# Fp32r pairs in place of fp32 products in the recurrence of an RWKV-7 mixer: bonus, spread of the key norms, and v by token

## The reference

```
kk = heads(k * k_k);  kk = kk / max(sqrt(sum(kk * kk, -1)), 1e-12)
k = k * (1 + (a - 1) * k_a)
y = wkv7_scan(r, decay, k, v, -kk, kk * a)     # S = S diag(w) + (S a) b^T + v k^T ; y = S r
yn = ((y - mean(y)) * rsqrt(var(y) + GN_EPS)) * lnx[0] + lnx[1]
bonus = sum(r * k * r_k, -1) * v               # per head
out = ((yn + bonus) * g) @ w_out
```

## Time and profile before

| | |
|---|---|
| median of 3 runs | 3334.22 us (3332.93 to 3335.73) |
| the profiled execution | 3333.84 us, its span 3332.1 us |
| PE busy | 98% of the span |
| DVE, ACT busy | 54%, 37% |
| mean granted PE clock | 0.994 |
| the stage of the pairs | from 2604 us to 2799 us of the span |

### The profile page before, as it was taken

The page is one execution under the profiler, slowest core; times in us unless marked ns, Lnnn a source line. Parts: engine busy times, 40 slices in busy tenths (PEclk is TensorE's granted clock), DMA queues, the critical chain, the costliest instruction groups (busy, mean ns, idle before and its releaser), DMA issues.

```text
span 3332.1 us, 46863 instructions
## 1 busy us (share of the span) xinstructions
PE 3253.6 (98%) x20502; PEld 2658.2 (80%) x20502; DVE 1783.3 (54%) x2116; ACT 1216.2 (37%) x1534; POOL 97.2 (3%) x100
## 2 busy tenths in 40 slices
PE   8999998999999999999999999999999999999998
PEld 6877786888878888988788887888777787788886
DVE  5446665777354434454644347443476665754437
ACT  3346643323232222343332235222235554332224
POOL 2000000000000001000100011000000000100001
PEclk9999999999999999999999999999999999999999
DMA  5211231222222222222222222222222100122231
GB/s 194 77 51 51 76 114 63 89 101 86 96 97 101 90 94 108 102 89 89 95 90 97 89 104 84 95 101 87 90 70 75 47 4 16 70 101 101 86 104 64
DMA packets 45979, 286.47 MB, mean 86 GB/s; under 512 B 5952, under 2 KB 6224, under 8 KB 19920
## 3 DMA queue, kind: packets, MB, share of 16 engines
q1 hardware_dynamic: 44240, 280.34, 23.9%
q0 software_dynamic: 1536, 3.15, 0.4%
HBM read 278.22 MB, written 2.10 MB: 84 GB/s over the span
## 4 chain that ended last, share of the span: by engine, by line
PE 79%; DVE 5%; ACT 2%; issue 1%; DVEq 0%; ACTq 0%
PE ps L510 70%; PE ps L3189 3%; PE ps L3227 1%; PE ps L1217 1%; DVE wl L331 1%; PE ps L983 1%; DVE xl L2663 1%; PE ps L1218 0%; PE ps L1219 0%; ACT wh L315 0%; PE ps L2493 0%; DVE xl L1077 0%; PE ps L837 0%; DVE tmp L2671 0%; PE ps L3234 0%
## 5 line engine op out<-in xcount | busy, mean ns | idle before, releaser
L510 PE MATMUL ps<-xh,wh 128*128 128x512 f32 (+1 forms) x2464 | 966.3, 392 | 22.4 <-DVE xl L1077 10.5
L510 PE MATMUL ps<-xl,wh 128*128 128x512 f32 (+1 forms) x2464 | 946.2, 390 | 0.3
L510 PE MATMUL ps<-xh,wl 128*128 128x512 f32 (+1 forms) x2464 | 920.5, 391 | 0.0
L331 DVE TENSOR_TENSOR wl<-raw,wh 128x2048 fp32r<-128x2048 f32 (+1 forms) x284 | 591.2, 2082 | 452.5 <-ACT wh L315 452.3
L315 ACT CAST wh<-raw 128x2048 fp32r<-128x2048 f32 (+2 forms) x281 | 487.6, 1735 | 296.5 <-PE ps L510 290.2
L510 PEld LDWEIGHTS ps<-xh,wh 128*128 128x128 f32 (+1 forms) x2464 | 462.6, 188 | 131.8 <-issue 27.8
L510 PEld LDWEIGHTS ps<-xl,wh 128*128 128x128 f32 (+1 forms) x2464 | 462.3, 188 | 100.7 <-DVE xl L1077 2.8
L510 PEld LDWEIGHTS ps<-xh,wl 128*128 128x128 f32 (+1 forms) x2464 | 461.9, 188 | 99.4 <-issue 1.0
L510 PE MATMUL ps<-hid_h,wh 128*128 128x512 f32 x880 | 342.8, 390 | 0.0
L510 PE MATMUL ps<-hid_l,wh 128*128 128x512 f32 x880 | 342.4, 389 | 0.0
L510 PE MATMUL ps<-hid_h,wl 128*128 128x512 f32 x880 | 342.4, 389 | 0.0
(11 more groups left out here) (424 smaller groups left out, 4015.2 us busy)
## 6 DMA issues: line engine op xcount, KB each, us to landing
raw<-in_up SPq DMA_DIRECT2D x88, 1024.0 KB, 4.7
raw<-in_down SPq DMA_DIRECT2D x64, 704.0 KB, 4.0
raw<-in_up_c SPq DMA_DIRECT2D x22, 1024.0 KB, 4.8
raw<-in_down_c SPq DMA_DIRECT2D x16, 704.0 KB, 4.1
raw<-in_gates SPq DMA_DIRECT2D x8, 1024.0 KB, 4.7
raw<-in_gv SPq DMA_DIRECT2D x8, 1024.0 KB, 4.7
raw<-in_gu SPq DMA_DIRECT2D x8, 1024.0 KB, 4.7
raw<-in_gout SPq DMA_DIRECT2D x8, 1024.0 KB, 4.7
```

The source lines that it names most:

```text
L331: nc.vector.tensor_tensor(wl[:, slot, 0:w], raw[:, slot, 0:w], wh[:, slot, 0:w].bitcast(F32), ALU.subtract).then_inc(lo_ready, 1)
L510: last = nc.tensor.matmul(out, stationary, moving, start=(fresh and q == 0), stop=(t == kt - 1 and half == per - 1 and q == 2), skip_group ...
```

## The change: what it does

- The three products become pairs of fp32r products: the table (0, 1 and 1/64 entries) rounded once, the data in a high and a low part. `bonus` and `spread` issue two fp32r products of 512 columns each, `tokens_v` eight of 128 columns, with the parts of v as the weights.
- The parts: per pair ScalarE gets `value_high` (behind `decays(m+1)`) and `terms_high` (behind `lower(m+1)`), VectorE gets `value_low` (behind `operand_k(m+1)`) and `terms_low` (behind `add_x(m, 1)`). All use the same two buffers `part_h`, `part_l`. The key norms are split once: ScalarE's copy waits for the reciprocal, VectorE's subtraction follows it, both in `between[0]` of rv2.
- The rounded tables are made by ScalarE in the lead part: `picks_r` (128x256) first, `sums_r` (128x256) last. `spread(0)` waits for the first, `tokens_v(0)` for the second.
- The four buffers of parts lie in the slot of `raw` that held the last chunk of rv2. The load of the first rout chunk into that slot is held until the last pair's `bonus` product; the loads queued behind it on SyncE wait with it.

```diff
-               split_ahead=False, second_ahead=False, joint=False, paired=False, third=False):
+               split_ahead=False, second_ahead=False, joint=False, paired=False, third=False, hold=False):
...
-            for n in range(a, a + count):
+            for n in range(a, a + count - 1 if hold else a + count):
...
+        halves_r = place("halves_r", [P, 4, T], F32R, offset=raw_at + other * SLOT * 4)
+        part_h, part_l, norms_h, norms_l = (halves_r[:, n, :] for n in range(4))
...
+            def value_low(m):
+                need(dve, aH, m, "v")
+                mark(nc.vector.tensor_tensor(part_l, tile(v, m), part_h.bitcast(F32), ALU.subtract), vH, "v")
+
+            def terms_low(m):
+                need(dve, aH, m, "rkr")
+                mark(nc.vector.tensor_tensor(part_l, tile(r, m), part_h.bitcast(F32), ALU.subtract), vH, "rkr")
...
+            def value_high(m):
+                if m:
+                    need(act, pA, m - 1, "bonus")
+                mark(nc.scalar.copy(part_h, tile(v, m)), aH, "v")
+
+            def terms_high(m):
+                need(act, vL, m, "rkr")
+                need(act, pA, m, "v_tok")
+                mark(nc.scalar.copy(part_h, tile(r, m)), aH, "rkr")
...
+                masks_here(act)
+                nc.scalar.copy(picks_r[:, :, :], const[:, CONST["pick_low"]:CONST["pick_high"] + P].rearrange(
+                    "p (a c) -> p a c", a=2)).then_inc(tables_made.sem, 1)
                 key_scale(0)
                 unscaled_keys(0)
                 decays(0)
+                value_high(0)
+                act.wait_ge(kn_norm.sem, kn_norm.base + 5)
+                nc.scalar.copy(sums_r[:, :, :], const[:, CONST["heads"]:CONST["centre"] + P].rearrange(
+                    "p (a c) -> p a c", a=2)).then_inc(tables_made.sem, 1)
...
-                mark(nc.tensor.matmul(ps[:, bank["spread"], :], table("pick_low" if m < 4 else "pick_high")[rows, :],
-                                      key_norms[rows, :], start=True, stop=True), pS, "spread")
+                out, picks = ps[:, bank["spread"], :], picks_r[rows, m // 4, :]
+                nc.tensor.matmul(out, picks, norms_h[rows, :], start=True, stop=False)
+                mark(nc.tensor.matmul(out, picks, norms_l[rows, :], start=False, stop=True), pS, "spread")
...
+                need(pe, vH, m, "v")
                 for j in range(PAIRS):
                     at_ = slice(j * P, (j + 1) * P)
-                    last = nc.tensor.matmul(ps[:, bank["v_tok"], at_], tile(v, m)[:, at_], table("centre"), start=True, stop=True,
-                                            skip_group_check=True)
+                    for n, part in enumerate((part_h, part_l)):
+                        last = nc.tensor.matmul(ps[:, bank["v_tok"], at_], part[:, at_], sums_r[:, 1, :], start=(n == 0),
+                                                stop=(n == 1), skip_group_check=True)
...
-                need(pe, vL, m, "rkr")
-                mark(nc.tensor.matmul(ps[:, bank["bonus"], :], table("heads"), tile(r, m), start=True, stop=True), pA, "bonus")
+                need(pe, vH, m, "rkr")
+                nc.tensor.matmul(ps[:, bank["bonus"], :], sums_r[:, 0, :], part_h, start=True, stop=False)
+                mark(nc.tensor.matmul(ps[:, bank["bonus"], :], sums_r[:, 0, :], part_l, start=False, stop=True), pA, "bonus")
...
-                pe.wait_ge(kn_norm.sem, kn_norm.base + 3)
+                pe.wait_ge(kn_norm.sem, kn_norm.base + 5)
+                pe.wait_ge(tables_made.sem, tables_made.base + 1)
                 spread(0)
...
+        def norms_of_keys_high(act):
+            root_keys(act)
+            act.wait_ge(kn_norm.sem, kn_norm.base + 3)
+            nc.scalar.copy(norms_h, key_norms[:, :]).then_inc(kn_norm.sem, 1)
...
+            dve.wait_ge(kn_norm.sem, kn_norm.base + 4)
+            nc.vector.tensor_tensor(norms_l, key_norms[:, :], norms_h.bitcast(F32), ALU.subtract).then_inc(kn_norm.sem, 1)
...
+        @block.sync
+        def _(sp):
+            sp.wait_ge(pA.sem, pA.done(KD - 1, "bonus"))
+            load(sp, first["rout"])
```

More of the change, by code:

```diff
@@ L237, in _build @@
     at[0] = (at[0] + LINE - 1) // LINE * LINE
+    raw_at = at[0]
     raw = place("raw", [P, 2, SLOT])
@@ L2761, in rwkv @@
         kn_square, kn_sum, kn_norm = roles("keys_squared", "keys_summed", "keys_normed")
-        for s, n in ((kn_square, KD), (kn_sum, 1), (kn_norm, 3)):
+        for s, n in ((kn_square, KD), (kn_sum, 1), (kn_norm, 5)):
             s.stage(1, n)
@@ L2845, in rwkv @@
         head_sums = area("head_sums", [P, 2, 32], 82 * KB + 512)
+        halves_r = place("halves_r", [P, 4, T], F32R, offset=raw_at + other * SLOT * 4)
+        part_h, part_l, norms_h, norms_l = (halves_r[:, n, :] for n in range(4))
+        sums_r, picks_r = area("sums_r", [P, 2, P], 80 * KB, F32R), area("picks_r", [P, 2, P], 82 * KB + 768, F32R)
+        tables_made, = roles("sum_tables_rounded")
+        tables_made.stage(2, 1)
         masks_here = fetch([(reset[:, :], io["reset"]), (masks[:, :, :].rearrange("p m c -> p (m c)"), io["wmask"]),
@@ L2852, in rwkv @@
         vA = Named(sem("grams_vector"), ["x0", "rb_t", "ak_t", "rk_t", "bonus"], KD, lead=True)
+        aH = Named(sem("highs_scalar"), ["v", "rkr"], KD, lead=True)
+        vH = Named(sem("lows_vector"), ["v", "rkr"], KD, lead=True)
         vB = Named(sem("levels_vector"), ["add1", "add2", "add3", "add4", "add5"], KD, lead=True)
@@ L3009, in pair_vector @@
             if lead:
-                for s in (vE, vL, vA, vB, vC):
+                for s in (vE, vL, vA, vB, vC, vH):
                     dve.sem_inc(s.sem, s.per)
@@ L3015, in pair_vector @@
                 unit_keys(0)
+                value_low(0)
                 return
@@ L3031, in pair_vector @@
                 add_x(m, 1)
+                terms_low(m)
                 bonus(m)
@@ L3038, in pair_vector @@
                     operand_k(m + 1)
+                    value_low(m + 1)
                 add_x(m, 3)
@@ L3130, in pair_scalar @@
             if lead:
-                for s in (aE, aA, aB, aC):
+                for s in (aE, aA, aB, aC, aH):
                     act.sem_inc(s.sem, s.per)
+                masks_here(act)
+                nc.scalar.copy(picks_r[:, :, :], const[:, CONST["pick_low"]:CONST["pick_high"] + P].rearrange(
+                    "p (a c) -> p a c", a=2)).then_inc(tables_made.sem, 1)
                 key_scale(0)
@@ L3142, in pair_scalar @@
             lower(0)
+            terms_high(0)
             key_scale(1)
@@ L3157, in pair_scalar @@
                     decays(m + 1)
+                    value_high(m + 1)
                 turned_x(m, 2)
@@ L3174, in pair_scalar @@
                     lower(m + 1)
+                    terms_high(m + 1)
                 if next_:
@@ L3334, in pair_tensor @@
             pe.wait_ge(psum_read.sem, values_read)
+            pe.wait_ge(tables_made.sem, tables_made.base + 2)
             tokens_v(0)
@@ L3399, in rates_and_keys @@
             invert_keys(dve)
-        linear("rv2", KD, 256, x_split, dve_part=to_tiles(v[:, 4:KD, :], 2),
-               between={0: (root_keys, rates_and_keys),
+            dve.wait_ge(kn_norm.sem, kn_norm.base + 4)
+            nc.vector.tensor_tensor(norms_l, key_norms[:, :], norms_h.bitcast(F32), ALU.subtract).then_inc(kn_norm.sem, 1)
+        linear("rv2", KD, 256, x_split, dve_part=to_tiles(v[:, 4:KD, :], 2), hold=True,
+               between={0: (norms_of_keys_high, rates_and_keys),
                         1: (lambda act: pair_scalar(act, True), lambda dve: pair_vector(dve, True))},
```

## The result

The changed kernel takes 3346.51 us (median of 4 runs, 3346.03 to 3348.39), the kernel before 3334.09 (4 runs, 3332.93 to 3335.73). The ratio is 1.004, 95% interval 1.0028 to 1.0051: 12.4 us slower, where 3334.1 was forecast, within 3330.0 to 3338.0. The profiled execution took 3348.39 us, its span is 3346.6, 14.5 more than before.

What follows compares the result with a forecast made beforehand. TensorE's queue was taken to bound the pairs (21.86 of 22.4 us busy). Later unit 1 +1.9, lower clock +1.6 and shorter pairs -3.6 gave -0.1 us on 3334.22: 3334.1 us, range 3330.0 to 3338.0.

Steps and rivals of the forecast that it cites:

- the last sentence on the covers: SyncE: first rout chunk loads at the last bonus, about 2773, each chunk taking 4.7 us, split at 2799.32; cost nothing.
- The products: In each pair, bonus and spread take 0.65 us each (0.41 and 0.40 less), tokens_v 1.09 (0.10 more).
- the wait that was named: At xt(2) TensorE waits 0.25 us for VectorE's add, so spread saves only 0.15 of 0.40 us.
- Pair 0: The first pair, waiting on ScalarE's z copies already, was taken to get 0.4 us shorter.
- The last pair's 0.41: Saving of 0.41 us in the last pair, which has no spread and no tokens_v behind its bonus.
- The covers on ScalarE and VectorE: Making the parts of the data, about 0.6 to 0.69 us each, hides in idle time or behind other work; cost nothing.
- the margin called the narrowest: On ScalarE, terms_high (0.6 us) hides in 0.47 us of idle before turned_x(0) plus 0.29 before the z(1) copy.
- The rival of ScalarE as the bound: terms_high and value_high not hidden, each adding 0.5 us a pair: 3340.7 us, half of it 3337.5; chance 0.13.
- that of the dear short products: Short fp32r products cost as long ones, tokens_v 0.93 us dearer seven times: 3339.9 us; chance 0.05.
- The head: At spread(0) in rv2, TensorE waits 2.4 us for picks_r, unit 1 starts 1.9 later; lower clock adds 1.6.
- The rival that the clock doesn't fall there: The clock stays up after the wait at spread(0), so 1.6 us less: 3332.5 us; chance 0.25.

Runs made afterwards that it cites:

- both mends: The changed kernel with picks_r made ahead of ScalarE's split of lora_g2 and the second rout chunk loaded ahead of the pairs: 3330.94 us, ratio 0.9991.
- the mend of the loads alone: The changed kernel with the second rout chunk loaded ahead of the pairs, only 1 MB left for the last bonus: 3334.35 us, ratio 1.0002.

## Why the prediction was wrong

**The step that failed** is the last sentence on the covers, "SyncE: the first rout chunk starts at the last bonus ... Nothing." I asked of the held loads only when their data are wanted, and that answer was right: the split of rout waits for VectorE as before. I didn't ask what else the 16 DMA engines carry while 2 MB pass. What the runs show in its place is +12.56 us: 2.47 of standing and about 10 at 1.2 GHz. The hold alone costs 11.9 us on the kernel before, and taking half of it away gives 3346.51 - 3334.35 = 12.2 back. All the rest of the sum would have made 3334.

That the stand is a late fetch of instructions is read, not shown by itself: the wait ends with "issue", q8 has no packet from 2776 to 2782, and in the three traces with two loads at once TensorE goes on 2.2 to 2.4 us behind the start of the delayed packet. The Trainium skill, "Runtime: NRT & Kernel Launch", section "Instruction fetch mechanics", says that each engine fetches its instructions in blocks of 16 KiB over a DMA queue of its own, and the q8 packets of 0.02 MB agree with the size. It calls the cost of crossing from one block to the next mostly hidden; here, with 2 MB of other traffic, a stand of 2.4 to 2.5 us isn't. No run here delays that queue by itself.

**The products.** Forecast 0.65, measured 0.66 for `bonus`. Its worth, from the kernel without it, is 22.20 - 21.82 = 0.38 us a pair, forecast 0.41. `spread`, worth 21.97 - 21.82 = 0.15, forecast 0.15: VectorE's add bounds it, and the wait that was named shows with 0.19 us. `tokens_v` was mis-sized: eight short fp32r products take 0.94 us, not 1.09; entry and exit hardly cost anything there. With the other changes around it that is 0.02 us a pair gained instead of 0.10 lost. So a steady pair is 22.37 - 21.83 = 0.54 us shorter, forecast 0.46.

**Pair 0** was wrong by as much the other way: -0.03 us where I took -0.4. In it `value_high` sits on ScalarE's path, as the 19.90 us without it shows. The two errors nearly cancel, by luck, and the stretch came out at -3.41, forecast -3.2. The last pair's 0.41 lies behind `bonus(7)`; with both mends only 0.13 of it shows.

**The covers on ScalarE and VectorE held.** `turned_x(4, 0)` has no idle left, and z(4, 1) behind it still 0.30 us, against the 0.47 and 0.29 of the earlier trace rows: the margin called the narrowest was used up and no more. The timeline of ACT of the kernel after:

```profile
2703.47 0.59 ACT L3143 COPY x_area<-ps 128x512 f32<-128x512 f32 x1
2704.36 0.60 ACT L3137 ACTIVATE x_area<-ps 128x512 f32<-128x512 f32 x1 [0.30 <-PE ps L3228]
```

The rival of ScalarE as the bound is refuted, and that of the dear short products as well.

**The head** was right in mechanism and size: 2.44 us of waiting (2.4), 1.66 of clock (1.6). Moving the copy takes it away: both mends together are 3.4 us faster than the mend of the loads alone. The rival that the clock doesn't fall there is refuted.

**The chances.** I gave 0.06 to "slower", all of it to ScalarE and the short products. That a stand brings the clock down I had priced at the head, with the earlier trace rows; the same price at a second place was open to me, had I found what makes TensorE stand there. It would have been too low even so: 2.47 + 1.6 is about 4 us, against 12.56, since the low clock lasts some 24 us there and 3 behind `spread(0)`.

**What stays open** is why the low clock lasts 17 to 24 us in the last pair and some 7 in pair 3. In both PE shows as busy. In the last pair the gate products of 512 columns stand among 64x64 ones, in pair 3 there are only the latter and transposes. No run separates this. Open too is why the stand of 2.16 us at 2422 is followed by a low clock in some executions and not in others.

## What to carry to other kernels

A load that is moved or held has two prices: when its data come, and what else shares the DMA engines while it runs; so look where the instruction queue has its packets, and spread the loads there while the bounding engine works (here 2 MB at once cost 12 us, 1 MB nothing that shows). On an engine that sets the end, a stand can cost several times itself by the clock (9.2 us for 2.36 here), so it is to be filled or avoided even where only one occurs. Price each edit of a set by taking it back alone, and compare stretch by stretch: here one of three gained 0.02 us in a steady pair, and of the 3.7 us between the two profiled spans nearly all lies where that edit does nothing.

## What the runs showed of the hardware

- Two loads of 1 MB at once went with a stand of TensorE of 2.47, 2.40 and 2.50 us on "issue" in three kernels; one load of 1 MB at the same place with 0.21. The packets of the instruction queue q8 were 7.0 to 7.2 us apart across the two loads, and 4.6 across the one.
- Stands of 2.36, 2.40, 2.44, 2.47, 2.50 and 3.68 us were each followed by a granted clock of 0.50; one of 2.03 us was not. One of 2.16 us, the same in all 15 traces, was in eight of them. The low clock lasted some 3 us behind `spread(0)`, among dense products of 512 columns, 7 us in pair 3, and 17 to 24 in the last pair, though PE was recorded as busy throughout.
- Eight fp32r products of 128 columns, each with weights of its own, take 0.94 us in all; two of 512 columns between fp32 products take 0.66.
- Nine fp32 products of 256 columns take 4.08 us, 0.45 each.
